# A two-block model in one program: other homes for three intermediate tensors, expert weights fetched in pairs and three chunks of them sooner

## The reference

```python
hx = rms_norm(x, pre_mix_g) * (1 + sc1) + sh1
b, c, u, q, k, v, g = split(hx @ w_in)                 # 7 parts of 512
y = retention(rotary(q), rotary(k), v, states of the context)   # 4 heads of 128
mu = mean(y, -1); var = mean((y - mu) ** 2, -1)
ret = silu(g) * ((y - mu) * rsqrt(var + eps)) * norm_g
mix = concat(conv(b, c, u), ret) @ w_out
x = x + g1 * rms_norm(mix, post_mix_g)

h = rms_norm(x, pre_ffn_g) * (1 + sc2) + sh2           # input of the experts
aff = softmax(h @ w_router + b_router)                 # (256, 16)
gate, idx = top_k(aff.T, 32)                           # 16 experts take 32 tokens each
for e in range(16):
    xs = h[idx[e]]                                     # (32, 1024)
    hid = silu(xs @ w_gate[e]) * (xs @ w_up[e])        # (32, 2048)
    y[idx[e]] += (hid @ w_down[e]) * gate[e]
x = x + g2 * rms_norm(y, post_ffn_g)
```

## Time and profile before

| | |
|---|---|
| time, 3 runs | 1599.95 us median (1598.51 to 1600.23) |
| profiled execution | 1600.5 us, its span 1598.7 us |
| PE busy | 1241.2 us (78%) |
| DVE, ACT, POOL busy | 614.4, 423.8, 37.4 us (38%, 27%, 2%) |
| DMA | 552.14 MB, mean 345 GB/s |
| chain that ended last | PE 44%, DMA 34%, DVE 13%, ACT 5%, issue 3% |
| loads of expert weights | 62 to 64 of each matrix at 2048 KB, 33 to 41 us from issue to landing |

### The profile page before, as it was taken

One profiled execution on the slowest core, in us unless ns is written; L12 is line 12 of the kernel. 1 busy time (PEld: TensorE's weight loads), 2 busy tenths in 40 slices (PEclk: granted clock), 3 DMA queues, 4 the chain that ended last, 5 costly groups with the idle time before them and its releaser, 6 DMA issues.

```text
span 1598.7 us, 17895 instructions
## 1 busy us (share of the span) xinstructions
PE 1241.2 (78%) x7202; PEld 684.8 (43%) x7202; DVE 614.4 (38%) x981; ACT 423.8 (27%) x640; POOL 37.4 (2%) x64
## 2 busy tenths in 40 slices
PE   5999999999999999776666667665666665665665
PEld 3788887877878798521111111111111111111111
DVE  2687789888667877510110110110110110110111
ACT  2566357786544754300000000000000000000000
POOL 1010000010000000000000000000000000000000
PEclk8999999999999999788877868788868888788888
DMA  9696777686656555899999999999999999999996
GB/s 347 240 298 225 254 259 239 242 299 228 217 184 217 172 177 193 345 426 430 427 427 428 428 428 426 429 428 427 428 427 428 428 427 428 428 428 428 428 428 270
DMA packets 91091, 552.14 MB, mean 345 GB/s; under 512 B 6440, under 2 KB 6760, under 8 KB 63232
## 3 DMA queue, kind: packets, MB, share of 16 engines
q1 hardware_dynamic: 87600, 541.09, 84.3%
q0 software_dynamic: 3120, 9.60, 1.9%
q10 hardware_dynamic: 288, 0.30, 0.1%
HBM read 549.87 MB, written 1.61 MB: 345 GB/s over the span
## 4 chain that ended last, share of the span: by engine, by line
PE 44%; DMA 34%; DVE 13%; ACT 5%; issue 3%; SPq 2%; POOL 0%; DVEq 0%; ACTq 0%
PE ps L566 41%; DMA b<-in_w_down 33%; DVE b L1347 6%; ACT b L1009 4%; PE ps L570 3%; DVE b L1364 2%; SPq L483 1%; DVE b L2014 1%; ACT b L1011 1%; DVE b L1982 1%; DVE b L1984 1%; DMA b<-in_w_ada 1%; DVE b L1355 0%; DVE b L1357 0%; DVE b L1378 0%
## 5 line engine op out<-in xcount | busy, mean ns | idle before, releaser
L566 PE MATMUL ps<-b,b 128*32 128x512 f32 (+4 forms) x6846 | 1181.5, 545 | 286.8 <-DMA b<-in_w_down 96.3
L566 PEld LDWEIGHTS ps<-b,b 128*32 128x32 f32 (+1 forms) x6846 | 638.6, 158 | 782.6 <-issue 265.6
L1009 ACT ACTIVATE b<-ps 128x512 f32<-128x512 f32 (+3 forms) x176 | 95.9, 545 | 885.9 <-PE ps L566 593.0
L1347 DVE TENSOR_TENSOR b<-b,b 128x1024 fp32r<-128x1024 f32 (+4 forms) x259 | 281.4, 1086 | 118.5 <-ACT b L1009 100.8
L1009 ACT ACTIVATE b<-b 128x1024 fp32r<-128x1024 f32 (+5 forms) x223 | 221.8, 995 | 236.6 <-PE ps L566 171.8
L2014 DVE TENSOR_TENSOR b<-b,ps 128x1024 f32<-128x1024 f32 x28 | 34.2, 1221 | 343.2 <-PE ps L566 343.2
L2004 DVE TENSOR_TENSOR b<-b,ps 128x512 f32<-128x512 f32 x16 | 11.0, 687 | 387.3 <-issue 370.7
L570 PE MATMUL ps<-b,b 128*128 128x128 f32 x356 | 70.9, 331 | 62.9 <-DVE b L1378 27.4
L570 PEld LDWEIGHTS ps<-b,b 128*128 128x128 f32 x356 | 47.1, 171 | 122.7 <-DVE b L1378 37.4
L1364 DVE SCALAR_TENSOR_TENSOR b<-b,b,b 128x512 f32<-128x512 f32 (+3 forms) x51 | 65.5, 1284 | 7.3 <-POOL b L2044 3.3
L1347 DVE TENSOR_TENSOR b<-ps,b 128x512 f32<-128x512 f32 (+8 forms) x69 | 37.6, 545 | 31.1 <-ACT b L1011 24.0
(11 more groups left out here) (52 smaller groups left out, 159.8 us busy)
## 6 DMA issues: line engine op xcount, KB each, us to landing
b<-in_w_gate SPq DMA_DIRECT2D x64, 2048.0 KB, 40.5
b<-in_w_up SPq DMA_DIRECT2D x64, 2048.0 KB, 41.1
b<-in_w_down SPq DMA_DIRECT2D x62, 2048.0 KB, 32.8
b<-in_w_in SPq DMA_DIRECT2D x74, 1024.0 KB, 5.2
b<-in_w_ada SPq DMA_DIRECT2D x28, 1024.0 KB, 5.1
b<-in_w_ada SPq DMA_DIRECT2D x16, 512.0 KB, 11.7
b<-in_w_proj_m SPq DMA_DIRECT2D x8, 1024.0 KB, 5.2
b<-in_w_out SPq DMA_DIRECT2D x8, 1024.0 KB, 5.0
```

The lines of the kernel that those rows point to most:

```text
L566: return e.matmul(o, lhsT, rhs, start=start, stop=stop, skip_group_check=True)
L1009: e.activation(o, i, f, bias=bias, scale=scale).then_inc(mark[0], 1)
L1347: e.tensor_tensor(o, a, b, op).then_inc(mark[0], 1)
```

## The change

It has six parts.

1. **Centred values.** The mean over channels is taken from the values `V` of context and latents before the retention, by one reduction each on DVE and eight ACT instructions each; the mean, subtraction and one step behind the retention go away. The output gate product comes one half earlier.
2. **Earlier decay tables.** `WT` and `wfb` are made during slot 29 instead of 34 to 39; `KF` in slot 36 instead of 39.
3. **Other homes.** `GX` moves to 43, `RY`/`RSQ` to 102/106, `RS`, `CVC`, `CVU` to 50, `WT` to 82, the last product `M` to 98 and 106 (KB in the arena); so places 66, 82 and 0 are empty once RV1 is full.
4. **No `H2`.** PE gathers rows of `X` itself. `ONE` carries the root of the norm (`hsq`) instead of 1, and DVE applies scale and shift to the turned rows `XT`, from two small tiles of 8 columns (SC8, SH8). For this the columns are split in another order: gather and gate/up products read their moving operand with a stride (`XC`, `hidden`).
5. **Residual and router** are cut into halves: `v_x2` counts twice for each half of the tokens, and flips and router products alternate.
6. **Weight loads.** Chunks 0 to 9 have ten places of their own; chunk 0 is issued as soon as RV1 is full, ahead of the last load of `w_out_2`, chunks 1 and 2 right behind that. From chunk 10 on two chunks are one load of 4 MB (8192 elements, 32 KB, of each partition) into four places of 32 KB, used in turn; a pair waits until the two chunks before in its place are used. The last pair is loaded in pieces. GG2 is loaded once `X` is final instead of after chunk 8.

```diff
-E_ORDER = (66, "HT", 82, "ring2", "ring0", "WS0", "WS2", 50, 16)
+E_ORDER = (66, 82, 0, "HT", "ring2", "ring0", "WS0", "WS2", 50, 34)
+E_PAIR_AT = (66, "ring0", "WS0", 34)
...
+        def expert_weight(n):
+            if n < E_FIRST:
+                return EW[n], (S(f"ew{n}"), 16)
+            m, g = (n - E_FIRST) // 2, n % 2
+            return EP[m % E_PAIRS][:, g * 4096:(g + 1) * 4096], (S(f"ew{m % E_PAIRS}"), 16 * (m // E_PAIRS + 2))
+        def pair_src(n):
+            e_, c = n // NCH, n % NCH // 2
+            if c < 4:
+                w_ = dram["w_gate"] if c < 2 else dram["w_up"]
+                return w_[e_, 512 * (c % 2):512 * (c % 2) + 512, :].rearrange("(p b) n -> p (b n)", b=4)
+            return dram["w_down"][e_, 1024 * (c - 4):1024 * (c - 4) + 1024, :].rearrange("(p b) n -> p (b n)", b=8)
...
+                e.wait_ge(S("p_use"), (2, 6, 8, 10)[m] if m < E_PAIRS else n - 2 * E_PAIRS + 2)
+                if m < pairs - 1:
+                    e.dma_start(EP[i], pair_src(n)).then_inc(S(f"ew{i}"), 16)
...
+            def hidden(w, b, n):
+                return w.rearrange("p (b c q g l) -> p b c g q l", b=2, c=2, g=2, l=4)[:, b, n // 2, n % 2]
...
-                        ins = mm(ps[32 * j:32 * j + 32, 0, 0:T], ONE[:, t, :], H2[:, t, j * T:(j + 1) * T], t == 0, t == NT - 1)
+                        ins = mm(ps[32 * j:32 * j + 32, 0, 0:T].rearrange("p (q l) -> p q l", l=2), ONE[:, t, :],
+                                 XC[:, t, j // 2, j % 2], t == 0, t == NT - 1)
...
-                copy(XT.rearrange("p a b -> p (a b)"), ps[:, 0, T:2 * T], to=S("a_xt"))
...
+                if (s, c) in ((37, 1), (39, 3)):
+                    i = 0 if s == 37 else 1
+                    e.wait_ge(S("v_vm"), i + 1)
+                    for n in range(NT * RH):
+                        v = (VC4, VX4)[i][:, n, :]
+                        act(v, v, ACT.Identity, bias=vmean[:, i, n:n + 1], to=S("a_v"))
...
+                reduce(vmean[:, i, :], (VC4, VX4)[i], ALU.add)
+                ts(vmean[:, i, :], vmean[:, i, :], -1.0 / RD, None, ALU.mult, to=S("v_vm"))
...
-                    reduce(gmean, RY4, ALU.add)
-                    ts(gmean, gmean, 1.0 / RD, None, ALU.mult)
-                    tt(RY4, RY4, gmean.unsqueeze(2).broadcast_to([P, NT * RH, RD]), ALU.subtract)
...
-                stt(X[:, t, :], M[:, t, :], v, X[:, t, :], ALU.mult, ALU.add, to=S("v_x2"))
+                for n in range(2):
+                    ns = slice(n * W, (n + 1) * W)
+                    stt(X[:, t, ns], M[t][:, ns], v, X[:, t, ns], ALU.mult, ALU.add, to=S("v_x2"))
...
-            def normed(t):
-                h = hsq[:, t:t + 1]
-                stt(H2[:, t, :], X[:, t, :], h, SC2R, ALU.mult, ALU.mult)
-                tt(H2[:, t, :], H2[:, t, :], SH2R, ALU.add, to=S("v_h2"))
...
-                    ins = e.tensor_scalar(ONE[:, t, :], iota[:, 0:CAP], rank[:, t:t + 1], None, ALU.is_equal)
+                    ins = e.tensor_scalar(ONE[:, t, :], iota[:, 0:CAP], rank[:, t:t + 1], hsq[:, t:t + 1], ALU.is_equal, ALU.mult)
...
+                e.wait_ge(S("p_xt"), x + 1)
+                e.tensor_tensor(xt, ps[:, 0, T:2 * T].rearrange("p (b j n) -> p b j n", b=2, j=4), four[0], ALU.mult).then_inc(S("v_xt"), 1)
+                e.wait_ge(S("v_xt"), 2 * x + 1)
+                e.tensor_tensor(xt, xt, four[1], ALU.add).then_inc(S("v_xt"), 1)
```

More of the change, by code:

```diff
@@ L535, in _ @@
             e.wait_ge(*full("WP1b"))
[L536 to L545 removed]
+            for n in (6, 7, 8):
+                expert_load(n)
+            e.wait_ge(*full(f"LG{NT - 1}"))
@@ new lines, in _ @@
+            expert_load(9)
+            pairs = (NE * NCH - E_FIRST) // 2
+            for m in range(pairs):
+                n, i = E_FIRST + 2 * m, m % E_PAIRS
+                e.wait_ge(S("p_use"), (2, 6, 8, 10)[m] if m < E_PAIRS else n - 2 * E_PAIRS + 2)
+                if m < pairs - 1:
+                    e.dma_start(EP[i], pair_src(n)).then_inc(S(f"ew{i}"), 16)
+            e.dma_start(EP[i][:, 0:4096], chunk_src(n)).then_inc(S(f"ew{i}"), 16)
+            for b in range(4):
+                bs = slice(b * D, (b + 1) * D)
+                e.dma_start(EP[i][:, 4096:][:, bs], chunk_src(n + 1)[:, bs]).then_inc(S(f"ew{E_PAIRS + b}"), 16)
@@ L721, in states @@
                 e.wait_ge(S("v_kf"), d + 1)
-                for name in ("CVa", "CVb"):
-                    e.wait_ge(*free(name))
+                e.wait_ge(S("a_v"), NT * RH)
                 for h in range(RH):
@@ L1817, in _ @@
                         modulate_lo(f"XF{q}", 9, HTL, HTH)
[L1818 to L1819 removed]
+                if s == 29 and 1 <= c < 5:
+                    h = c - 1
                     if h == 0:
@@ L2111, in _ @@
             power(9, gsq)
-            e.wait_ge(*full("RV1"))
-            e.memset(GT, 0.0).then_inc(S("g_work"), 1)
             for t in range(NT):
```

227 lines of the change are left out of this document (102 added, 125 removed).

## The result

The changed kernel takes 1587.35 us (median of 4 runs, 1585.06 to 1588.93) where the kernel before takes 1600.09 (4 runs, 1598.51 to 1601.93): 12.7 us less by the medians; the ratio is 0.9911, 95% interval 0.9893 to 0.9929, some 14 us less. The profiled execution took 1585.06, its span 1583.0. The forecast was 1585, with a range of 1579 to 1596.

The account below looks back on a forecast made before the run. The prediction took the experts to be bound by DMA transfer of their weights. From 1600.5 us it took 7.2 for the stream's start, 1.2 for GG2 and 7 for the rate: 1585.1, forecast 1585, range 1579 to 1596.

Parts of the forecast that it names:

- The bound: Experts bound by transfer of their weights: end is the unbroken stream's start, bytes left at the rate, plus an 18 us tail.
- The rate, -7 us: Experts' weight stream: 32 KB rows save half a fixed packet cost of about 9 ns per 16 KB, 428 to 431 GB/s.
- WP1b full, 659.7 to 654.4: Dense part: PE's 2.91 us wait at the retention output's flips goes, and about 2.4 us from the clock come back.
- costing the tables at nothing: Decay tables moved to slot 29, some 4 us of ACT: no cost; PE waits 1 to 2 us if the lead is used up.
- From WP1b to the first use: Router to first chunks: 13.9 us to the affinities become 9.6, then 7.1 plus 0.65 to first chunk, 6.1 to second used.
- The start, -7.2 us: Start of the unbroken expert stream from chunk 10 on: first bytes move at 679.6 instead of 686.8 us; bounds -3 to -9.7.
- the stream now really stops for a moment: Before the first pair: chunk 9 in by 677, pair issued at 677.8, its first bytes some 1.8 us later.
- GG2's 1.2 us: The load of GG2, before amid the saturated stream, now goes ahead of it: 1.2 us less.
- The tail: Behind the last byte, put at about 1580.5: 18 us to the end, the same after the change.
- Unchanged rate (1592): Rival: rate stays at 428 GB/s, rows split into 16 KB or fixed cost is the queue's; 1592 us, chance 0.20.
- Front without savings: Rival: clock falls anyway, another engine holds PE, or router chain stays as long; 1594 us, half of it 1590; chance 0.08.
- Strided reads: Rival: strided moving reads halve PE's gate and up rate, PE becomes the bound, 61 against 58.8 us; 1625; chance 0.03.

Follow-up runs that it names:

- the longer router: Changed kernel with 5 us of DVE work, its results unread, put between the norm and the router's logits; 1590.95 us, ratio 0.9938 to the kernel before.
- the late first chunks: Changed kernel with its first chunks issued at the moments of the kernel before; 1589.39 us, ratio 0.9921 to the kernel before.
- the old steps: Changed kernel with DVE work behind the retention in its old length and order, gate product one half later again; 1592.23 us, ratio 0.9948.
- the first profile: Profiled launch of the changed kernel in its original measurement, without edits; this execution took 1585.06 us, median of its runs 1587.35.
- the second profile: Profile of the changed kernel run once more without edits, as base for later runs; median 1587.3 us, ratio 0.9909 to the kernel before.
- 16 KB rows: Changed kernel with each pair of chunks loaded by two transfers of 2 MB instead of one of 4 MB; 1593.34 us, ratio 0.9947.

## Why the prediction was right, and where its steps were off

**The bound.** Right. The time is the start of the unbroken stream, its bytes at its rate, and the tail; what the longer router, the late first chunks and the old steps did to the start came through to the end of the span.

**The sum, and luck in it.** The sum gave 1585.1 for the profiled execution, and 1585.06 was measured, but that launch was the fastest of four and the one in which the stream did not stop. The median is 2.3 us above the forecast. By the packets of the traces, the moment at which 350 MB are still to move comes 9.9 us sooner in the first profile and 7.5 in the second; less GG2 and what the rate gives up to there (1.7), the start of the stream is 8.2 and 5.8 us sooner, around the 7.2 of the forecast. Since the front moves by up to 3 us between launches, agreement to a tenth is luck, while the size of each term is not.

**The rate, -7 us.** Right in mechanism and size. 16 KB rows cost 6.1 (ratio) or 6.7 us (within the profile). The fixed cost of 9 ns measured 9.3. But its source was misread: the stretch of the earlier trace rows did not hold 4 KB rows alone.

```profile
DMA packets 189, 0.97 MB, mean 405 GB/s; under 512 B 21, under 2 KB 21, under 8 KB 166
```

23 of the 189 packets carried 16 KB, more than a third of the bytes. With these taken out at 612.5 ns each, 4 KB take about 164 ns, the fixed cost comes out at 14 ns and the rate term at 10 us. That the uncorrected 160 led to 9 was luck.

**WP1b full, 659.7 to 654.4.** Measured 655.03, and the two terms are right: from the start of the half in front (630.80 before, 631.73 in the first profile) to WP1b full it is 28.9 us before and 23.3 now, 5.6 less, 2.9 of it the wait and 2.7 the clock (flips 1.97 to 1.04, the 60 matmuls behind them 15.89 to 14.22 us), where 2.9 and 2.4 were taken. The half in front, however, starts 0.9 later than before. Part of the tables moved to slot 29 can be seen on the way there: DVE is 9.26 of 10 us busy from 440 to 450 where it was 5.54, is 0.4 us late 30 us on, and PE, which comes sooner, waits 1.57 instead of 0.62 there. A stretch and PE's row before, then the same two after:

```profile
440.00:450.00 10.00, 10.00 (x46) 8.29 (x45) 5.54 (x6) 4.13 (x4) 0.00 (x0) 1.00 0.64 211
```

```profile
477.71 0.66 PE L570 MATMUL ps<-b,b 128*128 128x128 f32 x4 [0.62 <-DVE b L1347]
```

```profile
440.00:450.00 10.00, 10.00 (x46) 8.29 (x45) 9.26 (x12) 3.59 (x4) 0.00 (x0) 1.00 0.60 211
```

```profile
478.12 0.66 PE L567 MATMUL ps<-b,b 128*128 128x128 f32 x4 [1.57 <-DVE b L1362]
```

This wait of 1.57 stands in every profile with the changed front, but by itself it costs nothing at the end: from the group of matmuls in front of it to the half in front of the flips it is 159.4 us before and 159.4 to 159.5 in ten of the twelve profiles of kernels with the changed dense part, the old steps' kernel not counted. In the other two, the first profile among them, it is 160.8 to 160.9, and there the clock falls behind the wait. The same stretch in the first and in the second profile:

```profile
478.00:500.00 22.00, 21.25 (x93) 17.16 (x94) 15.96 (x19) 11.21 (x13) 3.09 (x5) 0.92 0.68 242
478.00:500.00 22.00, 19.64 (x93) 15.71 (x93) 17.94 (x21) 10.56 (x13) 3.09 (x5) 1.00 0.70 245
```

So costing the tables at nothing holds except in a launch in which the clock answers to the wait; then it is 1.5 us. That the tables cause the longer wait was read from the trace, not tried.

**From WP1b to the first use.** 13.9 us should become 9.6: it is 9.5 (655.03 to 664.51) in the first profile and 10.0 in the second, where the clock is lower. To the first chunk 7.8: it is 7.75. To the second use 6.1: it is 6.0 in the second profile and 3.7 in the first, at full clock.

**The start, -7.2 us.** The step "the stream now really stops for a moment" holds in each profile of this part but the first; there the landing of chunk 9 was the limit. I took that landing at 677; it was about 679, since four chunks and GG2 lie behind WP1b (20.8 us at 428 GB/s) and they move at 415 GB/s (660 to 677 us). The two limits are within 2 us of each other, which I did not see: it means that the router's saving and the sooner chunks each bring only what the other allows. GG2's 1.2 us hold: 1.4 at the end of the stream, 2.3 at the end of the span.

**The tail.** I put the last byte at 1580.5 by dividing the bytes of the last window by the full rate. The last piece is used at 1585.4: the last 5 us of the stream move at a share of 0.37 (1580 to 1586), not of 1. As it is the same in both kernels, the error cancels. The same reading gave 686.7 for the start of chunk 10; only differences of it were used.

**The rivals.** Unchanged rate (1592): the kernel with 16 KB rows is that case, and measured 1593.3. Front without savings: the longer router and the old steps are each a part of it, 1591.0 and 1592.2. Strided reads: right to look, wrong in price. I added up 21, 32 and 8 us for an expert, from rows of a PE that waits and so has half the clock for much of the time. A PE at work gets clock 0.91, its turn between experts shrinks to 17.4 us (1165.77 to 1183.20), and the stride costs a factor only at full clock: eight chunks take 29.1, not 32. PE is then still no bound, and a factor of 2.1 costs 11 us, not 33. In the changed kernel the reads cost nothing. (The 2.0 us that I gave for a chunk at full clock were a mean over both clocks: it is 1.74, 13.94 for eight.)

## What to carry to other kernels

Where a stream of loads is the bound, ask at its start which of two limits ends last, the landing of what is queued or the release of the next place, and by how much: a saving in one is worth only the distance to the other. Fixed costs of transfers can be had from two row sizes already in a trace, if each stretch holds one size alone (count its packets first), and a test with the rows halved checks them. A PE that idles before a stage can also slow the stage by its clock, so a wait removed is worth more than its length (here 5.6 us for 2.9); and one profile is one launch, with a clock state that the next may not have.
